# Two chained small operations in place of three in each pass of the level search of a sparse attention, and 12 unread matmuls in place of 37

## What is computed

```python
score = einsum('bths,bth->bts', relu(dots), wi * IDX_SCALE)
score = where(admissible, score, -inf)
_, sel = lax.top_k(score, n_sel)        # n_sel = 256 for the prompt
...
logits = einsum('btcgd,btkcd->btcgk', q, k_sel) * (A_HEAD_DIM ** -0.5)
logits = logits - slopes * dist
probs = softmax(logits)
out = einsum('btcgk,btkcd->btcgd', probs, v_sel)
```

## Time and profile before

| what | value |
|---|---|
| runs of before | 3041.67, 3034.4 and 3043.35 us; median 3041.67 |
| the profiled execution | 3042.04 us |
| its span in the trace | 3040.2 us |
| PE busy | 2951.2 us, 97% |
| DVE busy | 1697.6 us, 56% |
| ACT busy | 1146.5 us, 38% |
| POOL busy | 1382.4 us, 45% |
| mean granted clock of PE | 0.991 |

### The profile page before, as it was taken

How to read it: one execution, slowest core, us unless ns; L and a number is a source line. 1 busy time by engine, 2 the same in 40 slices (tenths; PEclk the granted TensorE clock), 3 DMA queues, 4 the chain that set the end, 5 groups by cost and what they waited for, 6 DMA issues and landing times.

```text
span 3040.2 us, 47623 instructions
## 1 busy us (share of the span) xinstructions
PE 2951.2 (97%) x18886; PEld 2770.1 (91%) x18886; DVE 1697.6 (56%) x3529; ACT 1146.5 (38%) x2437; POOL 1382.4 (45%) x963
## 2 busy tenths in 40 slices
PE   8999999999999999999989999999999999999997
PEld 8698778879999999999989999977899999999997
DVE  1898865544545554445764555565345544455466
ACT  2576554442223333333224554464312233333331
POOL 3131110045357787878322122212443778787771
PEclk9999999999999999999999999999999999999999
DMA  3021000112101111111222111111211111111121
GB/s 105 22 64 36 15 1 8 35 53 75 49 29 49 56 44 55 49 49 56 70 74 61 52 38 53 39 43 70 74 41 42 42 56 49 49 54 45 56 70 58
DMA packets 209455, 150.88 MB, mean 50 GB/s; under 512 B 28914, under 2 KB 195764, under 8 KB 209236
## 3 DMA queue, kind: packets, MB, share of 16 engines
q1 hardware_dynamic: 209236, 147.85, 16.3%
HBM read 128.09 MB, written 19.73 MB: 49 GB/s over the span
## 4 chain that ended last, share of the span: by engine, by line
PE 85%; DVE 8%; POOL 2%; issue 2%; ACT 2%; DMA 0%; PEld 0%; PEldq 0%; SPq 0%; DVEq 0%; ACTq 0%; POOLq 0%
PE psum L154 25%; PE psum L2516 24%; PE psum L2577 11%; PE psum L1830 6%; PE psum L715 4%; PE psum L2488 2%; PE psum L686 2%; PE psum L1399 2%; DVE junk L950 2%; PE psum L1367 2%; PE psum L697 2%; PE psum L1383 1%; PE psum L649 1%; POOL w_sum L2421 1%; POOL w_sum L2418 1%
## 5 line engine op out<-in xcount | busy, mean ns | idle before, releaser
L154 PE MATMUL psum<-x_hi,w_hi 128*128 128x352 f32 (+1 forms) x1464 | 482.2, 329 | 10.0 <-POOL x_lo L1792 4.1
L154 PE MATMUL psum<-x_hi,w_lo 128*128 128x352 f32 (+1 forms) x1464 | 473.6, 324 | 0.0
L123 POOL TENSOR_TENSOR w_hi<-w_raw,zeros 128x1024 fp32r<-128x1024 f32 (+1 forms) x77 | 128.9, 1673 | 757.3 <-PE psum L154 477.4
L154 PE MATMUL psum<-x_lo,w_hi 128*128 128x352 f32 (+1 forms) x1464 | 472.5, 323 | 0.0
L2373 POOL TENSOR_TENSOR w_lo<-w_raw,w_hi 128x512 fp32r<-128x512 f32 x264 | 351.5, 1346 | 218.0 <-ACT w_hi L2780 217.9
L2516 PE MATMUL psum<-x_hi,w_hi 128*128 128x352 f32 x1152 | 371.7, 323 | 0.0
L2516 PE MATMUL psum<-x_hi,w_lo 128*128 128x352 f32 x1152 | 370.3, 321 | 0.0
L2516 PE MATMUL psum<-x_lo,w_hi 128*128 128x352 f32 x1152 | 369.8, 321 | 0.0
L2373 POOL TENSOR_TENSOR w_lo<-w_sum,w_hi 128x512 fp32r<-128x512 f32 x216 | 294.6, 1382 | 0.0
L154 PEld LDWEIGHTS psum<-x_hi,w_hi 128*128 128x128 f32 (+1 forms) x1464 | 276.0, 189 | 12.2 <-issue 11.4
L154 PEld LDWEIGHTS psum<-x_lo,w_hi 128*128 128x128 f32 (+1 forms) x1464 | 276.8, 189 | 0.5
(11 more groups left out here) (647 smaller groups left out, 6861.0 us busy)
## 6 DMA issues: line engine op xcount, KB each, us to landing
w_raw<-in_ffn_w_dram SPq DMA_DIRECT2D x132, 512.0 KB, 3.8
w_raw<-in_b_w_in_dram SPq DMA_DIRECT2D x24, 512.0 KB
w_raw<-in_ple_w_gate_dram SPq DMA_DIRECT2D x16, 512.0 KB
x_nat<-in_x_prompt_dram SPq DMA_DIRECT2D x8, 512.0 KB, 7.9
w_raw<-in_a_w_in_dram SPq DMA_DIRECT2D x8, 512.0 KB
w_raw<-in_a_w_in_dram SPq DMA_DIRECT2D x16, 256.0 KB
x_rows<-x_rows SPq DMA_DIRECT2D x8, 512.0 KB, 2.8
out_new_b_v_prompt_dram<-valsB SPq DMA_DIRECT2D x8, 512.0 KB, 3.3
```

The source lines that it names most:

```text
L123: nc.gpsimd.tensor_tensor(c.w_hi[s][:, 0:kc], c.w_raw[s][:, 0:kc], zero, ALU.add).then_inc(c.split[s], 1)
L154: last = c.nc.tensor.matmul(out, w, x, start=(n == 0), stop=(n == 3 * len(terms) - 1))
```

## The change

In each pass the integers `tried`, a view of the column `missed`, now take `bits` xor 2^bit // 2: the trial level as it will be if the present bit stays. This copy is issued on DVE behind the last sweep, and needs no count. The comparison of `count` with `bound` writes 0 or 1 straight into `level_bits`, and the last operation shifts that by `bit` and puts it over `tried`. `s_top` counts one step fewer for the chain and one more for the copy, and the comparison waits for the copy too, since its wait is for all of `s_top` up to there. `FILL` goes from 37 to 12.

```diff
@@ mixer_a
-    bits = level[:, :].bitcast(I32)
+    bits, tried = level[:, :].bitcast(I32), missed[:, :].bitcast(I32)
...
-    FILL = 37
+    FILL = 12
...
@@ vector, in the pass of bit
-            done += ND
+            nc.vector.tensor_scalar(tried, bits, 2 ** bit // 2, None, ALU.bitwise_xor).then_inc(s_top, 1)
+            done += ND + 1
             v.wait_ge(s_top, done)
             v.wait_ge(s_signs, 2 * NA + NA * b + NA)
-            nc.vector.tensor_tensor(missed[:, :], count[:, :], bound[:, :], ALU.subtract).then_inc(s_top, 1)
+            nc.vector.scalar_tensor_tensor(out=level_bits[:, :], in0=count[:, :], scalar=1.0, in1=bound[:, :],
+                                           op0=ALU.mult, op1=ALU.is_lt).then_inc(s_top, 1)
             v.wait_ge(s_top, done + 1)
-            nc.vector.tensor_scalar(level_bits[:, :], missed[:, :], 0.0, float(2 ** bit), ALU.is_lt,
-                                    ALU.mult).then_inc(s_top, 1)
-            v.wait_ge(s_top, done + 2)
-            nc.vector.scalar_tensor_tensor(out=bits, in0=level_bits[:, :], scalar=2 ** bit // 2, in1=bits,
-                                           op0=ALU.bitwise_or, op1=ALU.bitwise_xor).then_inc(s_level, 1)
-            done += 2
+            nc.vector.scalar_tensor_tensor(out=bits, in0=level_bits[:, :], scalar=bit, in1=tried,
+                                           op0=ALU.logical_shift_left, op1=ALU.bitwise_xor).then_inc(s_level, 1)
+            done += 1
             v.wait_ge(s_level, b + 2)
```

## The result

| | before | changed |
|---|---|---|
| median, us | 3042.09 (16 runs, 3034.4 to 3047.38) | 3059.09 (16 runs, 3045.28 to 3065.81) |
| ratio | | 1.0047, 95% interval 1.0038 to 1.0056 |
| mean granted clock over all runs of the changed kernel | | 0.983 to 0.992 (0.984 in the slowest, 0.992 in the fastest) |
| profiled execution | 3042.04 us, span 3040.2 | 3045.28 us, span 3043.4 |
| search: first sweep to the end of the last L960 or L959 | 114.8 us | 118.8 us |

The change makes the kernel slower, by 14 us by the ratio and 17 by the medians. The runs of the changed kernel are spread over 20 us, and the one in its profile is the fastest. Six of the 16 runs take 3045.28 to 3053.68 us, with a mean granted clock of 0.989 to 0.992; ten take 3058.04 us or more, with 0.983 to 0.987.

The account below looks back on a forecast made before the run. PE holds 85% of the chain, but DVE paces 26 search passes. 3.3 us from the passes less 1.2 us lost to a clock fall gives 2.1 us gained: 3039.6 us from a median of 3041.67, range 3032.5 to 3044.0.

Parts of the forecast that it names:

- What paces the search, how many passes, what a pass without disturbance gains: Level search: DVE paces 26 passes, each 0.12 us shorter; with 0.20 from pass 4, 3.3 us gained.
- the 0.02 allowed: Search's small operations: margin of 0.02 us either way on the 0.20 step of an operation both reading and writing PSUM.
- The rule of the Trainium skill's page "VectorE: DVE Perf Modes" on the count of operations: Search's pass end: reduce operations rather than waits; with three small operations still, the pass would not be shorter.
- From above it costs a full step (nothing saved): Search's pass end: upper bound on the copy's cost, a full 0.20 us step; about 0.08 was taken.
- The row that I took as nearest: Small operation starting with an accumulator read at 327.28, its dependent 0.19 later; basis for the copy costing about 0.08 us.
- both go: PE's waits for ACT inside the search, 0.42 and 0.88 us, vanish, so projections end 1.3 us earlier, at 260.7.
- The gap before L686: Search's end: PE idle 2.5 us between the 12 filler matmuls and the last piece's reading, where it was 0.47.
- costing 3.4 x (1 - 0.16 / 0.29) = 1.5 us: Search's end: the gap puts PE at half speed for some 3.4 us; 1.2 us lost, between 0.8 and 1.6.
- a shift of that point as one of the end: Behind the search's end at 269.54 the chain is PE's, so moving that end moves the kernel's end equally.
- The rival on the other side: Search: copy costs a full step, 0.2 us saved, PE's gap 4.3 us, up to 1.6 lost: 3043.1 us, chance 0.12.
- nothing shows one: Search's copy: an integer operation on [128, 6] slower than 0.17 us would also make the kernel slower; no row showed it.
- The spread as bound of the range: Whole kernel: three runs of before, 3034.4 to 3043.35 us, used to set the range 3032.5 to 3044.0.

Follow-up runs that it names:

- experiment 2: Changed kernel with the copy writing to PSUM and the comparison to SBUF, 12 filler matmuls: 3056.77 us, ratio 1.0047.
- experiment 5: Changed kernel with the copy writing to PSUM and 27 filler matmuls: 3039.14 us, ratio 0.9993.
- experiment 12: Changed kernel with 37 filler matmuls and the copy as an operation with two inputs in SBUF: 3050.84 us in one run.
- experiment 11: Changed kernel with 37 filler matmuls and GpSimd's splits of the first attention in four instructions each: 3047.65 us in one run.
- experiment 1: Changed kernel again, without an edit: 3061.92 us, ratio 1.0057.
- experiment 4: Kernel before with 12 filler matmuls in place of 37: 3050.95 us, ratio 1.0029.
- experiment 8: Kernel before, 37 filler matmuls, with an added copy into PSUM that nobody reads in each pass: 3045.38 us, ratio 1.0024.
- experiment 9: Changed kernel with the copy into PSUM, 12 filler matmuls, and six unread matmuls ahead of the attention's 1.1 us wait: 3041.47 us, ratio 0.9994.
- experiment 10: Changed kernel with the copy into PSUM, 27 filler matmuls, and six unread matmuls ahead of the attention's 1.1 us wait: 3038.03 us, ratio 0.9981.
- experiment 13: Changed kernel as it is, with six unread matmuls ahead of the attention's 1.1 us wait: 3049.32 us, ratio 1.0021.
- experiment 14: Kernel before with 12 filler matmuls and six unread matmuls ahead of the attention's 1.1 us wait: 3046.19 us, ratio 1.0015.
- experiment 15: Kernel before with only six unread matmuls added ahead of the attention's 1.1 us wait: 3043.55 us, ratio 1.0004.

## Why the prediction was wrong

3039.6 us was forecast, with a range up to 3044.0; it came out at 3059.09, and the chance of slower by over 0.3% was given as 0.03. Point by point:

- **What paces the search, how many passes, what a pass without disturbance gains:** right. Comparison 0.20 behind the read, 0.12 less a pass, 3.53 to 3.54 us; where nothing holds the copy (experiments 2 and 5) the search is 111.3 us, 3.5 less than before, against 3.3 forecast. The comparison, reading and writing PSUM, takes 0.17 us, inside the 0.02 allowed. The rule of the Trainium skill's page "VectorE: DVE Perf Modes" on the count of operations, which would have saved nothing, did not hold for these: a third operation with no wait ahead of it costs 0.08 to 0.09. The section that the prediction names, "The DRAIN you can't avoid", adds itself that a next operation that is not held starts earlier; the prediction left that out.
- **"From above it costs a full step (nothing saved)": the first step that failed.** The copy costs 0.43 us in the mean and up to 2.10. The row that I took as nearest has the dependence right but a silent neighbour: GpSimd runs nothing between 300 and 340, while it has 30.15 us of work in the passes. And the three old operations gave no warning, since each touches PSUM: L955 reads it, L957 writes it, L960 reads it. The copy is the first small operation of the pass with both ends in SBUF. The Trainium skill says this outright ("SBUF — State Buffer", section "Who interferes with whom"): VectorE and GpSimd share one pair of ports as an exclusive lock. The Trainium skill also says there that a `tensor_scalar`, other than the form that writes out its accumulator, can enter a two-port mode that takes the pair, that an operation with two SBUF inputs contends with a GpSimd instruction that reads, and that whoever issues first blocks the other fully. The runs agree: 165 ns at most into PSUM (experiment 2), up to 2.10 us into SBUF (changed kernel), up to 2.02 with two inputs in SBUF (experiment 12), and only behind a split that had begun first. I had not weighed it for an operation of 0.17 us. The sign of the search's share turned there: 3.3 us gained became 4.1 lost.
- **PE's waits in the search "both go":** wrong for the same reason. The later one came to 3.00 us at 251.85. With the copy in PSUM, where no copy is held, it does go.
- **The gap before L686,** 2.5 us forecast: 3.69 in the changed kernel, 2.94 with the copy in PSUM. That it lowers the clock was right (0.74 in 270 to 275, 0.62 in experiment 2). Cutting the filler to 12 is more than the gain asks, also right; 27 leaves 0.62 us and costs nothing.
- **"costing 3.4 x (1 - 0.16 / 0.29) = 1.5 us", of which 1.2 went into the sum: the step that cost most.** It prices a fall once, at its place, and holds what follows for a mere shift ("a shift of that point as one of the end"). At its place the price was not far off: the attention takes 319.5 us with a fall of 3.4 us and 320.0 to 320.5 with one of 6.8, against 317.9, so 1.6 to 2.6 us. But with that fall the wait of 1.1 us for `ptA`, 30 us later, lowers the clock for 34.1 us in most runs: 14.1 us each time, more than nine times the price. The wait is in the kernel before as well, at 296.34 and 1.10 us long, and its clock stays up; in the 16 runs of the result and the 102 beside the experiments it never came to such a time. I had not looked at which waits behind the search would be marginal once the clock had been down. Nothing in the trace of before shows the price; its low places cost some 3.4 us of low clock each, for which the earlier trace rows stood.
- **The rival on the other side** had the short filler and the lost clock as its mechanism, and only the size of it, 1.6 us, was wrong. Its other half, a copy slower than its step, had "nothing shows one" against it.
- **The sum as it came out,** an estimate from these rows: 4.1 us of longer search, 1.6 to 2.6 of the fall at its place, 8.8 of the stretch as a mean over the 16 runs, 14.5 to 15.5 together. The means of the two kernels are 15.0 apart.
- **The spread as bound of the range:** the lowest and highest of three runs of before say nothing about a second group that the change itself opens.

What stays open is why the fall at the search's end makes the later one likely. By their times and granted clocks it came in four runs of four with the copy in PSUM and 12 filler matmuls, in ten of 16 of the changed kernel, in four of ten of before with 12 (two of them in part), and in none of 21 with the copy in PSUM and 27 or 20. One run had one of half the length without the first fall (experiment 11), so it isn't a condition. The traces hold one more hint. In the three profiles with the stretch of 34.1 us (experiments 1, 2 and 4) the fall at the search's end lasts 6.8 us, and the stretch starts 30.7 us behind its start. In the two profiles with a fall there, no six matmuls and no stretch (the changed kernel's first, experiment 8) it lasts 3.4 us. Whether the length of the first fall decides, or the distance, wasn't tried.

## What to carry to other kernels

An operation that is added to VectorE is priced with the neighbour that it will have: read from the trace what GpSimd does in that stretch, and if it works there, put the output of the small operation into PSUM or expect it to take as long as GpSimd's instruction under way. A gap of PE long enough to lower the clock is not priced at its own place alone: look through the next stretch of small matmuls for waits that the clock has just survived, and keep the gap short with a filler cut to what the gain needs (27 here, not 12; and where the search gets longer even 37 leave a gap, experiment 8), or fill the marginal wait itself (six matmuls, 1.2 us). And a profile of one execution can be the lucky one: where the runs lie in two groups, profile until both are seen.

## What the runs showed of the hardware

- A `tensor_scalar` on 128x6 integers from SBUF to SBUF, 0.17 us alone, is held by a GpSimd `tensor_tensor` that has begun before it, until that instruction ends: up to 2.10 us beside one of 2.40, and up to 0.68 beside ones of 0.74 and 0.61. With its output in PSUM it is never held (62 copies in experiments 2 and 8, 168 ns at most).
- The sweeps next to it are not held, though they read and write SBUF too: the one of 768 columns at 215.09 starts inside L123, takes 1.01 us across the start of L125, and takes the same at 211.55 with GpSimd idle. They are the form that also writes an accumulator, which the Trainium skill ("SBUF — State Buffer", section "Who interferes with whom") excepts, as these rows do.
- Around a wait of 1.1 us of PE the granted clock can fall to 0.50 for 34.1 us of work in which PE is busy all the time; the matmuls are small there (mostly 128x65 and 128x128), and no run tries it among larger ones. The same wait leaves it at 1.00 in other executions of the same kernel, and with six matmuls in its place the clock stayed at 1.00 in all five profiles and none of the 52 runs has the time and the clock of the stretch (experiments 9, 10 and 13 to 15).
- A few unread matmuls are cheap: six of 352 columns took 1.2 us inside a wait of 1.1, and the kernel before with them is unchanged (1.0004 [0.9994, 1.0014]).
